# Sparse attention of the odd layer by pairs of heads, with row-normalised weights and one PSUM sum for each tile

## The reference, cut to what matters

```
s_w = q.k * scale - slope * distance
p_w = masked_softmax(s_w, mask_w)
o_w = p_w @ v_w
o_n = gates[..., 0:1] * o_c + gates[..., 1:2] * o_s + gates[..., 2:3] * o_w
o_d = p_d @ v_d
out = concat([o_n, o_d]) @ w_out
```

## Time and profile before

| | us |
|---|---|
| median of 3 timed runs | 1462.5 (1462.34 to 1464.84) |
| profiled execution, its own time | 1471.16 |
| its span, first to last instruction | 1469.3 |
| TensorE matmul busy | 1413.2 (96%) |
| TensorE weight load busy | 1336.6 (91%) |
| VectorE / ScalarE / GpSimd busy | 751.3 / 501.1 / 404.6 |
| mean granted TensorE clock | 0.989 |

### The profile page before, as it was taken

How to read it: one execution, slowest core, us unless ns; L and a number is a source line. 1 busy time by engine, 2 the same in 40 slices (tenths; PEclk the granted TensorE clock), 3 DMA queues, 4 the chain that set the end, 5 groups by cost and what they waited for, 6 DMA issues and landing times. The chain is left out here.

```text
span 1469.3 us, 27103 instructions
## 1 busy us (share of the span) xinstructions
PE 1413.2 (96%) x11095; PEld 1336.6 (91%) x11095; DVE 751.3 (51%) x1378; ACT 501.1 (34%) x992; POOL 404.6 (28%) x478
## 2 busy tenths in 40 slices
PE   6999998999999999999899989999999999999996
PEld 5999975899999999999799867888999999999996
DVE  3425767577334343345689755434485343343435
ACT  3322124355213132133532445665454033130311
POOL 3014523464011020027735471022663010010102
PEclk9999999999999999999999989999999999999998
DMA  4343070031313213122421153202133132231301
GB/s 151 119 112 115 30 230 6 3 115 58 116 60 114 103 70 115 58 65 63 125 37 38 51 178 105 59 1 58 61 112 116 58 115 100 74 115 58 115 30 59
DMA packets 87195, 123.84 MB, mean 84 GB/s; under 512 B 24438, under 2 KB 42302, under 8 KB 87040
## 3 DMA queue, kind: packets, MB, share of 16 engines
q1 hardware_dynamic: 82048, 107.00, 22.7%
q0 software_dynamic: 5024, 15.10, 3.4%
HBM read 115.62 MB, written 8.57 MB: 85 GB/s over the span
## 5 line engine op out<-in xcount | busy, mean ns | idle before, releaser
L1034 PE MATMUL ps<-xh,ring_lo 128*128 128x260 f32 (+2 forms) x2496 | 505.2, 284 | 1.4 <-ACT big L1609 1.4
L1034 PEld LDWEIGHTS ps<-xh,ring_lo 128*128 128x128 f32 (+2 forms) x2496 | 384.0, 187 | 3.3 <-ACT big L1609 2.3
L1034 PE MATMUL ps<-xh,wr 128*128 128x260 f32 x1568 | 354.3, 285 | 6.5 <-POOL ring_lo L780 2.8
L1034 PE MATMUL ps<-xl,wr 128*128 128x260 f32 x1568 | 351.8, 283 | 6.1 <-DVE xl L2070 3.9
L1034 PEld LDWEIGHTS ps<-xh,wr 128*128 128x128 f32 x1568 | 256.7, 188 | 9.3 <-issue 5.0
L1034 PEld LDWEIGHTS ps<-xl,wr 128*128 128x128 f32 x1568 | 255.8, 188 | 8.2 <-DVE xl L2070 5.1
L833 POOL TENSOR_TENSOR att<-att 128x520 f32<-128x520 f32 (+1 forms) x80 | 77.3, 967 | 548.6 <-DVE att L1996 521.5
L1972 DVE TENSOR_TENSOR ring_lo<-ring,wr 128x1024 fp32r<-128x1024 f32 (+1 forms) x144 | 191.9, 1336 | 64.4 <-ACT wr L1609 64.2
L1034 PE MATMUL ps<-hh,wr 128*128 128x260 f32 x1024 | 222.1, 283 | 0.0
L1034 PE MATMUL ps<-hh,ring_lo 128*128 128x260 f32 x1024 | 221.8, 283 | 0.0
L1034 PE MATMUL ps<-hl,wr 128*128 128x260 f32 x1024 | 221.7, 283 | 0.0
(11 more groups left out here) (354 smaller groups left out, 1727.3 us busy)
## 6 DMA issues: line engine op xcount, KB each, us to landing
ring<-in_w_up SPq DMA_DIRECT2D x16, 2048.0 KB, 8.1
ring<-in_w_down SPq DMA_DIRECT2D x16, 2048.0 KB, 7.9
ring<-in_w_in_e SPq DMA_DIRECT2D x9, 1024.0 KB, 5.5
ring<-in_w_in_e SPq DMA_DIRECT2D x2, 2048.0 KB, 8.7
ring<-in_w_out_e SPq DMA_DIRECT2D x2, 2048.0 KB, 9.7
ring<-in_w_in_o SPq DMA_DIRECT2D x16, 256.0 KB, 5.0
ring<-in_cache_kv POOLq DMA_DIRECT2D x32, 128.0 KB, 2.4
ring<-in_w_out_o SPq DMA_DIRECT2D x8, 512.0 KB, 8.3
```

The costliest lines, as they stand in the source:

```text
L1034: last = pe.matmul(bank(g, half)[0:width(g), 0:H2], w[:, k, :], x[:, k, cols(half)], start=first, stop=final)
```

## The change

- Units are taken as pairs (g = 0 and g = 1 of one tile, `p` and branch). `turns` and `last_turns` now give two units of one job in a row; the jobs and their number stay.
- `pair_scores`: each head's scores are a matmul on its own 64 rows (partitions 0 to 63 or 64 to 127) of queries and keys, straight from `big`; g = 0 into `ps[0]`, g = 1 into `ps[1]`, issued in turn in chunks of at most two blocks. `KZ`, the padding on GpSimd and its memset are gone.
- `normalised`: once a pair, VectorE takes the reciprocal of the two sums, caps it, multiplies by the gate, and scales the two units' `Pb` by it, 128 x 128n each. The transposes wait for that.
- `pair_values`: V is stationary (128 rows, 64 columns) and the turned weights move (128 columns a block); the output is already channels by queries, g = 0 in partitions 0 to 63 and g = 1 in 64 to 127 of one bank, the two in turn block by block. All branches of a tile add up in that bank, the compressed one (formerly `final_begun`) first.
- `job_done`, `otok`, the d transposes, `final_added` and its wait in `tail` are gone. `final_out` copies the job's own bank at t = last unit + 5.
- Buffers: `Pb` six (was four), `PTb` four (was two); the pipeline is two to three steps longer.

```diff
-        turns = [0, 1] * NH
+        turns = [0, 0, 1, 1] * NP
@@ GpSimd
-            pool.memset(kiz[:, :, :], 0.0)
-            pool.memset(att[:, 0:3072], 0.0).then_inc(sm["z_pool"], 1)
-            pool.wait_ge(sm["z_pool"], 1)
+            pool.memset(kiz[:, :, :], 0.0).then_inc(sm["z_pool"], 1)
...
-            padded(0, "kd")
...
-            padded(1, "ks")
...
-            padded(2, "kw")
@@ TensorE
-                mm(ps[u % 2][:, 0:P * (i + 1 - k0)], big[:, L[f"q{'d' if br == 'd' else 'n'}{p}"], P * i:P * i + P],
-                   KZ["k" + br][:, g, P * k0:P * (i + 1)]).then_inc(sm["q_mm"], 1)
+                ends = sorted({min(i + 1, k0 + 2), i + 1})
+                for c0, c1 in zip([k0] + ends, ends):
+                    for g in range(2):
+                        if u >= 2 and c0 == k0:
+                            pe.wait_ge(sm["q_sc"], u + g - 1)
+                        r = slice(HD * g, HD * g + HD)
+                        last = mm(ps[g][:, P * (c0 - k0):P * (c1 - k0)], big[r, q, P * i:P * i + P],
+                                  big[r, L["k" + br], P * c0:P * c1])
...
             def unit_turned(u):
-                pe.wait_ge(sm["q_e"], u + 1)
+                pe.wait_ge(sm["q_n"], u + 1)
...
-                    last = mm(ps[5 + o % 2][:, c:c + HD], PTb[u % 2][:, P * b:P * b + P], v,
-                              start=(b == 0), stop=(b == i - k0))
+                    for g in range(2):
+                        r = slice(HD * g, HD * g + HD)
+                        v = tm[:, k0 + b, P * VS[br] + HD * g:P * VS[br] + HD * g + HD]
+                        last = mm(held_by(o)[r, P * p:P * p + P], v, PTb[(u + g) % 4][:, P * b:P * b + P],
+                                  start=(br == "d" and p == 0 and b == 0), stop=(b == i - k0))
...
+                if t % 2 == 0 and t + 2 < len(units):
+                    pair_scores(t + 2)
+                if t % 2 == 0 and 2 <= t <= len(units):
                     unit_turned(t - 2)
-                if 1 < t + 1 < len(units):
-                    unit_scores(t + 1)
-                if 0 <= t - 3 < len(units):
-                    unit_values(t - 3)
+                    unit_turned(t - 1)
+                if t % 2 and t >= 5:
+                    pair_values(t - 5)
@@ VectorE
-            def job_done(o):
+            def normalised(u):
+                r = rrec[u // 2 % 2]
+                dve.wait_ge(sm["q_e"], u + 2)
+                link(dve.reciprocal(r, rsum[o % 4][:, 2 * p:2 * p + 2]))
...
+                for g in range(2):
+                    dve.tensor_scalar(Pb[(u + g) % 6][:, 0:n], Pb[(u + g) % 6][:, 0:n], r[:, g:g + 1], None,
+                                      ALU.mult).then_inc(sm["q_n"], 1)
...
+                if t % 2 and 3 <= t < len(units) + 3:
+                    normalised(t - 3)
+                for f in range(2 * QT - 1):
+                    if t == last_of[last_job[f]] + 5:
+                        final_out(f)
```

More of the change, by code:

```diff
@@ L574, in build @@
         m8s = piece(8)
-        nmx = [piece(1) for _ in range(4)]
+        nmx = [piece(1) for _ in range(6)]
         rsum = [piece(NH) for _ in range(4)]
-        rrec = [piece(NH) for _ in range(2)]
+        rrec = [piece(2) for _ in range(2)]
         nms, rss, rcs = piece(1), piece(1), piece(1)
@@ L631, in build, with held_by @@
             last_of[x[5]] = u
-        def otok_of(o):
-            return otok[jobs[o][1], o % 2]
-        def final_jobs(f):
-            i, kind = FINALS[f]
-            return [o for o, (n, br) in enumerate(jobs) if n == i and (br == "d") == (kind == "d")]
-        def final_bank(f):
-            return ps[7] if f == len(FINALS) - 1 else ps[4]
+        last_job = [max(o for o, (n, br) in enumerate(jobs) if n == i and (br == "d") == (kind == "d")) for i, kind in FINALS]
+        def held_by(o):
+            return ps[5 + o % 2]
         cm = mixc
@@ L921, in kv_page @@
                 return lambda r: kv_rows[bass.ds(r, 1), :, c0:c0 + 256].rearrange("n p x -> p (n x)")
-            def padded(n, name):
-                tile_ready(name)
-                for g in range(2):
-                    pool.tensor_copy(KZ[name][HD * g:HD * g + HD, g, :],
-                                     big[HD * g:HD * g + HD, L[name], 0:S]).then_inc(sm["kz_ok"], 1)
-                    pool.wait_ge(sm["kz_ok"], 2 * n + g + 1)
-            padded(0, "kd")
             for name in O_NAMES[Z["qd0"]:Z["vw"] + 1]:
@@ L1366, in cached_keys @@
                         pe.wait_ge(sm["pct_ev"], 1)
-                    if st == 0 and n0:
-                        pe.wait_ge(sm["q_of"], 2 if n0 == 4 else 4)
                     for b in range(2):
@@ L1522, in final_begun @@
-            def final_begun(f):
-                i, kind = FINALS[f]
-                for p in range(NP):
-                    mm(final_bank(f)[:, P * p:P * p + P], VCb[:, p, :], PcT[:, P * i:P * i + P], start=(p == 0))
-            def final_added(f):
-                o = final_jobs(f)[-1]
-                pe.wait_ge(sm["q_g"], o + 1)
-                for p in range(NP):
-                    last = mm(final_bank(f)[:, P * p:P * p + P], otok_of(o)[:, p, :], ident[:, :], start=False)
-                last.then_inc(sm["of_mm"], 1)
@@ L1563, in _ @@
             pe.wait_ge(sm["free_a"], G_OUT1)
             pe.wait_ge(sm["free_b"], G_OUT1)
[L1565 to L1566 removed]
+            pair_scores(0)
             for s, name in enumerate(SLOTS):
@@ L1901, in compressed_step @@
                     copy(PcT, ps[4][0:64, :]).then_inc(sm["pct_ev"], 1)
-            for t in range(len(units) + 2):
+            for t in range(len(units) + 4):
                 if t < len(units):
@@ L2666, in _ @@
                     dve.wait_ge(sm["q_mm"], t + 1)
[L2667 to L2673 removed]
+                    if t >= 6:
+                        dve.wait_ge(sm["q_t"], t - 5)
+                    dve.tensor_tensor_reduce(Pb[t % 6][:, 0:n], tab, ps[g][:, 0:n], -SLOPE[NP * g + p], 3e38,
+                                             ALU.add, ALU.min, nmx[t % 6]).then_inc(sm["q_sc"], 1)
+                if t % 2 and 3 <= t < len(units) + 3:
[3 more added lines that the diff above has]
+                        final_out(f)
                 compressed_step(t)
                 sample_queries(t)
[L2676 to L2680 removed]
                 if t >= START and (t - START) % EVERY == EVERY - 1:
```

142 lines of the change are left out of this document (39 added, 103 removed).

## The result

The changed kernel took 1515.71 us (median of 4 runs, 1514.07 to 1517.37) against 1463.67 (4 runs, 1462.34 to 1469.84) for the kernel before: a ratio of 1.035, with an interval of 1.031 to 1.038. It is slower by 52 us. The forecast was 1450, and its range ended at 1479.

A forecast was written before the change was run, and what follows sets the result against it. TensorE was taken as the bound, matmuls filling 96% of the span. The attention stage's 8.4 us and GpSimd's 4.0 made 12.4 us, so 1462.5 - 12.4 = 1450 us; range for eight times in ten 1434 to 1479.

The forecast's parts named there:

- Overlap of scores and values: Attention stage: a pair's two half-array matmuls run at once, saving 14.7 us on scores and 16.6 on values.
- Both signs named for it: Trace of the stage: four-block pairs' scores and values about 1.07 us each; g = 1 starts before g = 0 ends.
- Switches: TensorE in the attention stage: three changes of array shape a pair at 0.12 us each, costing 17.3 us.
- Finals: Sums of four n finals, one in the tail, and 16 d-final transposes are gone, saving 5.8 us.
- GpSimd: Ahead of the low part: without memset and first copy, TensorE's wait and low clock go, gaining about 4.0 us.
- VectorE: Attention stage: busy time grows from 95.4 to 131 us of about 185, not the bound on average.
- the third rival: Attention stage: VectorE becomes the bound, as scalings cost more and TensorE waits for them; 1461 us, chance 0.14.
- The waits: Attention stage: 1.8 and 1 us off for its first 34 us, 5.6 for `final_out`, 3 for pipe fill and emptying.
- The term for `final_out`: VectorE's copy holds up the next pair's scores: TensorE waits 0.8 us, seven times, 5.6 us in all.
- The rival on the slow side: Attention stage: fp32 matmuls on half arrays run one after another; 17 us slower, 1479 us, chance 0.16.
- the chain that ended last: Profile of the kernel before: said to agree that only shortening TensorE's stream or its waits moves the end.
- the 1.8 us of saving taken off for the first eight pairs: Stage's first 34 us: 8 of the 48 pairs gain nothing there, so their share, 1.8 us, is taken off.

The follow-up runs named there:

- The streams: Kernel before with separate streams of TensorE work put ahead of the odd attention, without gaps or with gaps of 0.32 to 3.4 us; clock without gaps 1.00.
- The mixture: Stream added to the kernel before: the change's three-block pair (scores, six transposes, values, three switches of shape) in turn; repeats every 2.47 us.
- late: Changed kernel with the sample's operations and `final_out` two steps later in VectorE's queue: 1475.06 us, again 1477.29, ratio to before 1.0047.
- unscaled: Changed kernel without the 96 scalings of the weights on VectorE, so its outputs differ: 1502.33 us.
- scores_only: Kernel before with only the scores changed: on 64 rows in pairs, without the padded copies: 1491.43 us, ratio 1.0132.
- late_fill: late plus one full-array multiplication of 128 columns before each unit's transposes: 1468.02 us, then 1470.63, ratio to before 1.0018.
- late_fill_half: late_fill with the added multiplications on 64 rows instead of the full array: 1496.95 us, ratio 1.0205.
- fill_full: Changed kernel plus two multiplications of 128 columns on 128 rows before each unit's transposes: 1523.73 us.
- fill_half: fill_full with the added multiplications on 64 rows instead of 128: 1586.85 us.

## Why the prediction was wrong

- **Overlap of scores and values (31.3 us): right.** 1.06 us for a four-block pair of scores where 1.07 was forecast; 1.02 for values where 1.07 was. The streams gave even less for the values. Both signs named for it came out as forecast.
- **Switches (17.3 us), called the likeliest error: right in size.** The mixture took 2.47 us where 2.7 was due. In all, TensorE's work in the stage fell by 18.8 us by the estimate above and by 28 by the same estimate from `late`, where 19.8 was forecast. So the terms of the work held together, or were too small.
- **Finals (5.8 us): one part too small.** The last one, in the tail, was counted with 1 us; the tail is 4.2 us shorter.
- **GpSimd (4.0 us): 3.0 measured.** The wait and the lower clock behind it are both gone, as forecast. That nothing else is late was wrong: VectorE's four copies, now beside GpSimd's low parts, make TensorE wait 1.22 us.
- **VectorE: right that it isn't the bound** (131.7 busy us, 131 forecast), and so the third rival fell. Scalings of 384 columns took 0.75 us a pair against 0.72; `unscaled` shows that all of them are worth 13 to 19 us. In places the rival's mechanism is there: at 1006.23 two scalings of 256 columns beside a low part of GpSimd's took 2.71 us instead of 0.62, and TensorE waited 1.91.
- **The waits: the step that failed.** The forecast took off 11.4 us (1.8 + 1 + 5.6 + 3) and looked at `final_out` and the two ends only. TensorE's idle time rose by 32.6. The term for `final_out` held: TensorE waited 0.5 to 0.9 us at four of the seven copies, near the 0.8 named as its sign, 2.6 us in all where 5.6 was forecast. What had no term were the other operations in VectorE's queue: the sample's steps stand there ahead of a pair's scores and wait for TensorE's later work (10.7 us), the placing of the sample queries held TensorE for 4.91 us where 2.27 was reckoned to stay, and the transposes waited 15.8 us for scalings and copies. The change issues a pair's scores two steps ahead into the only two banks, so a late operation on VectorE stops TensorE at once. I had counted how long VectorE is busy, not what stands in its queue ahead of the scores. `late` shows the queue's order as cause: 44 of the stage's 59 us with the order changed. Pairs in two banks aren't enough: `scores_only` has them, issued one step ahead, and 6.8 us idle. Which part of the longer pipe adds the rest, no run shows.
- **The clock: a term that was missing.** 45 us by the estimate, some 9 us either way. The rows had shown it: 34 us at 0.85 and waits of 2 us behind which matmuls took twice as long. I used it as a sign of a rival, and put no price on what my own 11.4 us of waits would do to it. Nor did I ask if work on half the array holds it. `late_fill` and `late_fill_half`, `fill_full` and `fill_half`, 26 and 63 us apart, and `scores_only`, with no more idle time than before, show that the shape has a part. The Trainium skill, page TensorE: Matmul & The Clock Gate, section A second HAM failure mode: psum-queue depth-cycling, tells of a kernel whose small waits between groups of matmuls, as banks are taken in turn, made the clock go up and down. The trace agrees (0.72, 0.90, 0.59 in three stretches), though in the streams waits of 0.32 us alone left it at 1.00; that rule should have been a rival.
- The rival on the slow side (no overlap, 1479) gave the right sign by a mechanism that isn't there, and was still 37 us short.
- Two smaller slips: the chain that ended last was called a witness for the whole kernel, but it covers 26% of the span and begins at 1081 us, behind the stage; and the 1.8 us of saving taken off for the first eight pairs come to 2.6 by the forecast's own prices. Neither decides anything.

What stays open: how the 45 us divide between the waits and the shape in the changed kernel itself, and why paired row halves fell to 0.63 in `scores_only` with TensorE hardly idle, when they held 1.00 in the streams. The pairs are short there and stand between other work; the first instruction of the pair's first half and the last of its second run alone. The other work is a second candidate: much of it is the sample's, on 32 rows or columns or with eight moving columns, and no stream had it beside paired halves. Either reason is argued, not shown. A version with paired scores that run at full clock and without waits, which by the table would have a stage of some 170 to 180 us (an estimate, the work plus the 6 us idle of before), wasn't found.

## What to carry to other kernels

Price a change of TensorE's work at both levels of its clock: here 19 us of work were saved and 52 us of time lost, since each new wait and each lone half-array matmul can hold it at 1.2 GHz, where it looks fully busy. Before batching an engine's issues to every second step, read the queue of the engine that frees the banks, and list what stands there ahead of the operation that frees them and whom it waits for. If a wait can't be removed, changing the order of issue is the cheap first trial: here it gave back three quarters of the loss.

## What was not expected of the hardware

- fp32 matmuls on two column halves overlap with their loads: 0.215 us for 64 + 64 columns of weights and 128 moving columns each, against 0.21 for one value block on the full array.
- Lone row halves hold the clock at 1.00 without gaps, and fall to 0.55 with gaps of 0.32 us that leave row pairs, column pairs, transposes and full-array work at 1.00.
- More work can take less time: with about 20 us of full-array matmuls added, the kernel went from 1477.3 to 1470.6 (medians of 9 and 10 runs). The stages of the two profiled executions are 217.8 and 213.4.
- Four copies of 32x512 on VectorE took 1.76 us with GpSimd idle and 5.94 beside its low parts.
- Transposes hold the clock as matmuls do: 1.00 in a stream of them without gaps and with gaps of 0.32 us. The Trainium skill, page TensorE: Matmul & The Clock Gate, section PE-mode transpose, says that the full clock doesn't engage for them; the measurement differs, and decides.
